# Adding the last residual of a decoder layer by accumulating transfers into the output's rows

## The reference

```
x   = x + rms_norm(mixed @ w_out, norm_mix_post)          # h
hm  = rms_norm(x, norm_mlp_pre)
act = square(relu(hm @ w_up))                             # 1024 x 4096
x   = x + rms_norm(act @ w_down, norm_mlp_post)           # the output
rms_norm(y, g) = y * rsqrt(mean(y*y) + 1e-6) * g
```

## Time and profile before

| what | value |
|---|---|
| median of three executions | 1154.75 us |
| lowest and highest | 1152.32 and 1155.97 us |
| the profiled execution: time | 1152.76 us |
| the profiled execution: span | 1151.0 us |
| TensorE busy / VectorE / ScalarE / GpSimd | 98% / 68% / 35% / 5% |
| mean granted TensorE clock | 0.996 |

### The profile page before, as it was taken

The page is one execution under the profiler, slowest core; times in us unless marked ns, Lnnn a source line. Parts: engine busy times, 40 slices in busy tenths (PEclk is TensorE's granted clock), DMA queues, the critical chain, the costliest instruction groups (busy, mean ns, idle before and its releaser), DMA issues.

```text
span 1151.0 us, 14008 instructions
## 1 busy us (share of the span) xinstructions
PE 1122.8 (98%) x5110; PEld 908.4 (79%) x5110; DVE 785.3 (68%) x1127; ACT 399.2 (35%) x728; POOL 52.7 (5%) x94
## 2 busy tenths in 40 slices
PE   7999999999989999999999999999999999999996
PEld 6888887777756788878888888888888888888885
DVE  6666765756577546888867667766766666766768
ACT  7433933545567326642212112212221211211222
POOL 0300001000121110000000000000000000000010
PEclk9999999999999999999999999999999999999998
DMA  6111323111010456111121011110211102111062
GB/s 229 56 37 36 136 84 89 58 37 38 21 35 19 148 182 200 73 37 74 37 73 36 36 73 36 45 64 36 73 36 41 69 36 73 36 36 73 37 234 113
DMA packets 23397, 83.11 MB, mean 72 GB/s; under 512 B 3088, under 2 KB 3216, under 8 KB 23232
## 3 DMA queue, kind: packets, MB, share of 16 engines
q1 hardware_dynamic: 17424, 62.92, 15.3%
q0 software_dynamic: 5648, 19.60, 5.0%
q10 hardware_dynamic: 288, 0.09, 0.0%
HBM read 70.02 MB, written 8.39 MB: 68 GB/s over the span
## 4 chain that ended last, share of the span: by engine, by line
PE 89%; DVE 5%; DMA 2%; ACT 1%; issue 1%; SPq 0%; POOL 0%; DVEq 0%; ACTq 0%
PE pair L352 27%; PE pair L354 27%; PE pair L353 27%; PE pair L725 3%; PE pair L760 2%; DMA raw<-weights 2%; PE pair L742 1%; PE pair L728 1%; DVE y_gain L2087 1%; PE pair L574 1%; DVE yacc L2072 1%; DMA q_rot<-q_sb 1%; DVE h_sb L2101 1%; DVE negmax L1657 0%; DVE wl L1478 0%
## 5 line engine op out<-in xcount | busy, mean ns | idle before, releaser
L354 PE MATMUL pair<-wdh,xl 128*128 128x512 f32 x480 | 186.7, 389 | 0.0
L352 PE MATMUL pair<-wdh,xh 128*128 128x512 f32 x480 | 186.7, 389 | 0.0
L353 PE MATMUL pair<-wdl,xh 128*128 128x512 f32 x480 | 186.7, 389 | 0.0
L1883 DVE TENSOR_TENSOR yacc<-yacc,pair 128x1024 f32<-128x1024 f32 x104 | 127.0, 1221 | 80.2 <-PE pair L354 80.2
L1378 ACT ACTIVATE up_h<-raw 128x384 fp32r<-128x384 f32 x56 | 27.4, 513 | 226.9 <-DMA raw<-weights 226.9
L353 PEld LDWEIGHTS pair<-wdl,xh 128*128 128x128 f32 x480 | 90.1, 188 | 18.7
L352 PEld LDWEIGHTS pair<-wdh,xh 128*128 128x128 f32 x480 | 90.1, 188 | 18.7
L354 PEld LDWEIGHTS pair<-wdh,xl 128*128 128x128 f32 x480 | 90.1, 188 | 18.7
L352 PE MATMUL pair<-xh,wh 128*128 128x512 f32 x256 | 102.2, 399 | 1.0 <-DVE xl L1501 1.0
L354 PE MATMUL pair<-xh,wl 128*128 128x512 f32 x256 | 99.9, 390 | 0.0
L353 PE MATMUL pair<-xl,wh 128*128 128x512 f32 x256 | 99.7, 389 | 0.0
(11 more groups left out here) (305 smaller groups left out, 2099.1 us busy)
## 6 DMA issues: line engine op xcount, KB each, us to landing
raw<-weights SPq DMA_DIRECT2D x74, 512.0 KB, 3.3
wd_f<-weights SPq DMA_DIRECT2D x28, 512.0 KB, 3.6
x_sb<-x SPq DMA_DIRECT2D x8, 512.0 KB, 7.7
q_rot<-q_sb POOLq DMA_DIRECT2D x32, 128.0 KB, 2.7
out<-h_sb POOLq DMA_DIRECT2D x8, 512.0 KB, 3.5
h_sb<-out POOLq DMA_DIRECT2D x8, 512.0 KB, 11.2
out<-h_sb SPq DMA_DIRECT2D x7, 512.0 KB, 2.6
x_a<-x POOLq DMA_DIRECT2D x4, 512.0 KB, 6.8
```

Source lines behind the costliest of these rows:

```text
L352: pe.matmul(o, a_hi, b_hi, start=first, stop=False)
L353: pe.matmul(o, a_hi, b_lo, start=False, stop=False)
L354: return pe.matmul(o, a_lo, b_hi, start=False, stop=last)
L1883: dve.tensor_tensor(y, y, pair[2 + t % 2][:, :], ALU.add).then_inc(y_added, 1)
```

## The change

The seven whole tiles 0 to 6 are no longer read back and added on VectorE. After each norm ScalarE multiplies `y_gain` by `rstd` of the row into `h_sb` (a new activation of 128x1024, `fin_scaled`), and GpSimd's queue issues a transfer with `accum_op=ALU.add` that adds this tile to the output's rows in DRAM, where h has been since the first residual. `h_sb` of tile 7 alone is read back. In ScalarE's program the new activations stand behind the root of their norm and ahead of the next tiles' squares; they wait for `rstd` through a new semaphore. Tile 7's gain is made in two halves: the first stands behind tile 6's norm and ahead of the second half's sum. Its two half residuals and stores stay as they were. GpSimd waits for its seven transfers at the end, SyncE for its two.

```diff
@@ SyncE
-            for t in range(TT - 1):
-                sp.wait_ge(fin_done, t + 1)
-                sp.dma_start(out[0, P * t:P * t + P, :], h_sb[:, t, :]).then_inc(stored, 16)
             t = TT - 1
-            sp.wait_ge(fin_done, TT)
+            sp.wait_ge(fin_done, 1)
...
-            sp.wait_ge(stored, 16 * (TT + 1))
+            sp.wait_ge(stored, 16 * 2)
@@ GpSimd
-            for t in range(TT):
-                pool.dma_start(h_sb[:, t, :], out[0, P * t:P * t + P, :]).then_inc(h_back[t], 16)
             pool.wait_ge(h_stored, 16 * TT)
+            t = TT - 1
+            pool.dma_start(h_sb[:, t, :], out[0, P * t:P * t + P, :]).then_inc(h_back, 16)
+            for t in range(TT - 1):
+                pool.wait_ge(fin_scaled, t + 1)
+                pool.dma_start(out[0, P * t:P * t + P, :], h_sb[:, t, :], accum_op=ALU.add).then_inc(out_added, 16)
+            pool.wait_ge(out_added, 16 * (TT - 1))
@@ ScalarE, behind the root of norm n
+                if n < len(last_norms) - 1:
+                    act.wait_ge(fin_rstd, n + 1)
+                    for t in pair_:
+                        act.wait_ge(fin_gained, t + 1)
+                        act.activation(h_sb[:, t, :], y_gain[:, t, :], ACT.Copy,
+                                       scale=rstd[:, 3, t:t + 1]).then_inc(fin_scaled, 1)
@@ VectorE
-                rsqrt_post(var[:, ts], root[:, ts], t1[:, ts], t2[:, ts], rstd[:, 3, ts])
+                rsqrt_post(var[:, ts], root[:, ts], t1[:, ts], t2[:, ts], rstd[:, 3, ts], fin_rstd)
+            def last_half_gain(hf):
...
+                dve.tensor_tensor(y_gain[:, t, cols_], yacc[t // 4][:, t % 4, cols_], g_out[:, cols_],
+                                  ALU.mult).then_inc(half_gained, 1)
...
                 last_norm(n)
-                for t in last_norms[n]:
-                    last_residual(t, slice(0, D), fin_done)
-            t = TT - 1
+            last_half_gain(0)
             last_half_sum(1)
-            dve.wait_ge(half_added, 1)
-            last_gain(t)
+            last_half_gain(1)
             last_norm(len(last_norms) - 1)
-            last_residual(t, slice(0, HALF), fin_done)
-            last_residual(t, slice(HALF, D), fin_half)
+            last_residual(0, fin_done)
+            last_residual(1, fin_half)
```

More of the change, by code:

```diff
@@ L313, in build @@
         h_stored = sem("h_stored")
-        h_back = [sem(f"h_back{t}") for t in range(TT)]
+        h_back = sem("h_back")
         t_raw = sem("t_raw")
@@ L342, in build @@
         fin_done = sem("fin_done")
+        fin_rstd = sem("fin_rstd")
+        fin_scaled = sem("fin_scaled")
+        half_gained = sem("half_gained")
+        out_added = sem("out_added")
         fin_half = sem("fin_half")
@@ L2095, in last_norm, with last_residual @@
                 dve.wait_ge(fin_root, n + 1)
-                rsqrt_post(var[:, ts], root[:, ts], t1[:, ts], t2[:, ts], rstd[:, 3, ts])
-            def last_residual(t, cols_, signal):
-                dve.wait_ge(fin_gained, t + 1)
-                dve.wait_ge(h_back[t], 16)
+                rsqrt_post(var[:, ts], root[:, ts], t1[:, ts], t2[:, ts], rstd[:, 3, ts], fin_rstd)
+            def last_half_gain(hf):
+                t = TT - 1
+                cols_ = slice(HALF * hf, HALF * hf + HALF)
+                if hf == 0:
+                    dve.wait_ge(half_added, 1)
+                else:
+                    dve.wait_ge(y_added, 8 * MERGED + t + 1)
+                dve.tensor_tensor(y_gain[:, t, cols_], yacc[t // 4][:, t % 4, cols_], g_out[:, cols_],
+                                  ALU.mult).then_inc(half_gained, 1)
+            def last_residual(hf, signal):
+                t = TT - 1
+                cols_ = slice(HALF * hf, HALF * hf + HALF)
+                dve.wait_ge(half_gained, hf + 1)
+                dve.wait_ge(fin_rstd, len(last_norms))
+                dve.wait_ge(h_back, 16)
                 dve.scalar_tensor_tensor(h_sb[:, t, cols_], y_gain[:, t, cols_], rstd[:, 3, t:t + 1],
```

## The result

The changed kernel takes 1155.31 us (median of 20), the one before 1153.87 us (median of 20 beside it): ratio 1.0014, 95% interval 1.0008 to 1.0021. Forecast was 0.25% less; it is 0.14% more. That is under the 0.3% named in the prediction, but the interval leaves out 1, and the sign is the other one.

What follows compares the result with a forecast made beforehand. TensorE bounds the kernel until 1141.15 us, leaving a 9.85 us tail; 2.62 us from (a) and 0.32 from (b, c) make 2.94, so 1154.75 - 2.94 = 1151.8 us, 0.25% less. Range 1149.0 to 1159.5 us.

Steps and rivals of the forecast that it cites:

- Step (f): GpSimd's queue: last of seven accumulating stores lands at 1145.85, end 1146.3, hidden behind 1148.06 with 1.8 us to spare.
- The sign that the prediction gives for being right: At the end: GpSimd's last wait is over before SyncE's, the last accumulate landing near 1145.8 us.
- T: Time for which one accumulating store on GpSimd's queue fills the 16 engines; taken as 3.0 us, bounds 1.5 and 8.
- Rival 1: GpSimd's queue: accumulates set the end, T between 3.9 and 4.8; median 1154.6 at T = 4.3; chance 0.11.
- 7 us or more: Sign of being wrong on GpSimd's queue: accumulates land that long after issue, one queueing behind the other.
- Rivals 2 to 4: Accumulate queue with T over 4.8, slower (0.17); ScalarE's copy 1 us late, 1152.8; VectorE not freed, 1154.75; last two 0.06.
- (a): VectorE before the end: seven residuals of 1.28 us leave, tile 7's second half sum starts at 1141.18, 2.62 us gained.
- (b, c): Tile 7's tail: gain in halves, ScalarE's scaled copies of 1.16 us; mean squares added at +1.60, 0.32 us gained.
- (d): After the mean squares' sum nothing changes: 1.39 us to first residual, 1.44 to second issue, 2.45 to end.
- (e): Seven of eight read-backs and SyncE's seven stores go; the read-backs' absence is worth nothing, TensorE having no gap.

Runs made afterwards that it cites:

- e1: The changed kernel with SyncE instead of GpSimd waiting for the seven accumulates at the end; 1152.20 us, ratio 0.9988 to before.
- e3: The changed kernel with plain stores in place of the seven accumulates, so output tiles 0 to 6 lack h; 1152.01 us, ratio 0.9987 to before.
- e2: The kernel before, with a wait for SyncE's last stores added at the end of GpSimd's program; 1159.04 us, ratio 1.0039.
- e4: The changed kernel with tile 6 read back, added on VectorE and stored by SyncE, accumulates for tiles 0 to 5; 1151.43 us, ratio 0.9982 to before.
- e7: The changed kernel with accumulates only for tiles 0 to 3, tiles 4, 5 and 6 finished as before; 1151.68 us, ratio 0.9987 to before.
- e8: e7 with tile 7's first half gain moved into VectorE's wait for the root of tile 6; 1151.57 us, ratio 0.9980 to before.
- e6: e4 with tile 7's first half gain moved into VectorE's wait for the root of tile 6; 1152.26 us, ratio 0.9988 to before.
- e10: The kernel before, with GpSimd's program held open until tile 7's first half sum is done; 1154.18 us, ratio 1.0005.
- e5: The kernel before with only tile 7's gain made in two halves; 1153.77 us, ratio 1.0002.

## Why the prediction was wrong

**Step (f) failed, in one number.** It says: "landed 1.0 + 3.0 + 0.4 later at 1145.85, end 1146.3. That hides behind 1148.06 with 1.8 us to spare." The 0.45 us from a landing to the end had been read at SyncE's last store, and I put it behind GpSimd's too. It is 5.5 us there: 0.2 to leave the wait, 5.13 of DRAIN, 0.2 for the meeting. The sign that the prediction gives for being right, a last wait of GpSimd that is over before SyncE's, even held (1149.3 against 1150.6); the time lay behind the wait. The rest of the step was short by less: the issue comes 0.30 us behind the copy and not 0.04, and landing takes 5.3 us and not 4.4. With these two the accumulate lands 1149.3 - 1143.45 = 5.85 us behind the last matmul, against a forecast of 4.7; with 0.45 us behind it even that would have hidden in the 6.9 us of the forecast's tail. With 5.5 us it is the 11.35 measured. e1 and e3 take the landing and the DRAIN apart, and e2 makes the DRAIN without an accumulate. The DRAIN's row was in the trace of before, hidden under matmuls. That 1155.31 us still lies within the range of 1149.0 to 1159.5 is luck: the range was kept wide for the size of T.

**The rivals.** Rival 1 ("the accumulates set the end") is nearest, and names the wrong place: it wanted T of 3.9 us or more and a queue that backs up. T was 3.0 to 3.2 us. The queue did back up for a while: up to 8.3 us to landing, against the "7 us or more" that the prediction names as a sign of being wrong. But it had run dry again at the end, and the last accumulate was issued at 1144.0, when the one before it (issued at 1137.8, 5.4 us to landing) had landed. No rival had a price for the closing of GpSimd's program. Rivals 2 to 4 did not come about.

That T met its forecast of 3.0 is in part luck. The prediction read eight full slices in the bytes of a plain store and made it 1.5 us; the row has seven between two small ones, and the same view's line of the queue gives 18.4% of 7 us, 1.3 us:

```profile
q0 software_dynamic: 144, 0.52, 18.4%
```

Twice that would have been 2.6 us.

**What held.** (a) The residuals' leaving puts the second half sum behind the last matmul: 2.65 to 0.04 us, 2.62 forecast. (b, c) The mean squares are added 1.49 us after the half sum's start, not 1.60: the second half square starts 0.09 us after the first's accumulator read, overlapping it, so the copy ahead of them costs 0.03 and not 0.14 us. The copies take 1.15 us; 1.16 forecast. (d) 1.46 + 1.44 us to the last issue; forecast 1.39 + 1.44. (e) The missing read-backs were worth nothing: TensorE has no gap either way (23.20 of 23.20 us). The half stores' landing grew by 0.7 us beside the accumulate, for which the prediction had no term; beside plain stores (e3) it was 2.1 us. By its DRAIN at 1150.7 us, SyncE alone would have ended the changed kernel near 1151.0 us (an estimate, with the 0.2 us that followed it before), a tail of 7.5, 2.3 us under before. Most of what was forecast was there until the last engine closed.

**On the rule about reductions.** An accumulate fills the engines for 3.0 to 3.2 us, a plain store for 1.3 us. That is 2.3 to 2.5 times. The Trainium skill ("Collectives: The Full Stack", section "The bandwidth ceiling") gives half the speed for a reduce-scatter, because it reads two sources; the factor here is somewhat above two.

## What to carry to other kernels

Before a transfer is moved to the end of a kernel, ask of each engine what it still runs after its last wait, and look it up at the block's closing line; here GpSimd needs 5.1 us there, SyncE 7 ns. So in this kernel the last wait belongs on SyncE, and GpSimd's program should end more than 5 us before the others. If it must issue late, let another engine wait for its transfers; that gave 2.9 us here (e1), though the DRAIN then still ended 2.6 us behind the last landing. And relief counts only up to the point at which the late engine keeps pace: four tiles of seven gave the tail of six (7.77 and 7.83 us). The seventh brought the half sum on time, but not the kernel's end, since its accumulate, with the DRAIN behind it, came last.

## What the runs showed that I had not expected

- GpSimd's DRAIN at the closing takes 5127 ns when nothing is open (in the changed kernel, e2, e3, e4, e7, e8, e6 and e10, whatever went before it), and with transfers of its own still open it ends 2.6 us behind the last landing (before, e5 and e1). The closing DRAINs of the others in the changed kernel are 4267 ns on TensorE's queue, from 1139.2, 1289 on VectorE, 231 on ScalarE and 7 on SyncE. The Trainium skill ("VectorE: DVE Perf Modes", section "The DRAIN you can't avoid") tells of DRAINs of about 12 ns on all five engines, from what the runtime puts ahead of and behind a kernel. Those at this kernel's own line 74 are much longer, except for SyncE's.
- An issue by GpSimd takes 0.86 us for an accumulate of a tile and 0.53 us for a plain one, and the first bytes come some 1.4 us after it, so that the landing is 5.3 us for some 3 us of transfer. Why the start takes longer than a plain store's was not tried.
- Which part of the DRAIN's 5127 ns is fixed in any kernel, and which comes from the transfers that this one issued earlier, stays open: every version here issues over fifty of them on GpSimd.
